# Second layer's modulation: all 48 rows on VectorE during the first feed-forward, instead of 16 on TensorE in the filter stage

## The chip, the cores and the metric

The kernel runs on one core of a Trainium2 chip. The metric is the device time of one execution in microseconds. The core has five engines that run their own instruction streams in order and meet at semaphores: PE (TensorE, matmuls), DVE (VectorE), ACT (ScalarE), POOL (GpSimd) and SP (SyncE, which here only issues transfers). Transfers are also issued by ACT and POOL.

## The reference, cut to what matters

Two layers over 512 latent and 256 context tokens of width 1024. Each layer takes six modulation vectors per stream from the conditioning vectors: one matrix-vector product per stream with a 1024 x 6144 matrix.

```python
sc = jax.nn.silu(c)
scc = jax.nn.silu(c_ctx)
for layer in range(DEPTH):
    mod_l = jnp.split((sc @ ada_w[layer] + ada_b[layer])[:, None, :], N_MOD, axis=-1)
    mod_c = jnp.split((scc @ ada_w[layer] + ada_b[layer])[None, None, :], N_MOD, axis=-1)
    h_l = rmsnorm(x, norm1_g[layer]) * (1.0 + mod_l[1]) + mod_l[0]
    h_c = rmsnorm(ctx, norm1_g[layer]) * (1.0 + mod_c[1]) + mod_c[0]
    # layer 0: SSD + Hyena mixer; layer 1: windowed attention
    x = x + mod_l[2] * o_l
    h_l = rmsnorm(x, norm2_g[layer]) * (1.0 + mod_l[4]) + mod_l[3]
    x = x + mod_l[5] * swiglu(h_l, ffn_w_in[layer], ffn_w_out[layer])
    # the same for ctx in layer 0
```

With features on partitions, the 6144 values of a layer are 48 columns of 128 ("rows" of the modulation in the kernel's words), each for two streams. Layer 0's Hyena mixer also needs a filter that depends on no activation (a small MLP, a window, a norm and a Fourier-like transform). The kernel makes it first; here this is called the filter stage.

## The kernel before, in words

Weights come as a list of jobs of 1 MB (two halves of 512 KB, in three slots of SBUF, job g in slot g mod 3). SP loads the halves in the order of the list, and each load waits until PE has finished the same half of the job three places earlier. The order of the list is written out by hand in `weight_jobs`.

The kernel multiplies in float32 by splitting each weight and each activation into a high and a low part. For each half of a job DVE casts the weights to the high part (`split_high`, line 1704, called from `next_high`), POOL subtracts to get the low part (`low`, line 2255), and PE does three products for each tile (lines 530, 531, 535). There is one buffer for the high parts of a job's two halves. So DVE may cast half 0 of the next job only when PE has finished half 0 of this one, and PE needs the cast and POOL's subtraction by the time it has finished half 1.

The modulation is made in two ways:

- As jobs called "ada". A pair of them (2 MB) gives four columns for both streams, by 8 skinny matmuls with a 32-column stationary operand (function `ada`, line 597). Layer 0's 12 pairs are made so, and also the first 16 columns of layer 1, in 4 pairs. Eight pairs are made one after another inside the filter stage, at calls of `fill()`: after each of the three MLP layers, after the sixth tile of the first half of the filter (`c` is 0 or 1 for the two halves of 512 columns), after the second and the sixth tile of the second half, and twice in the transform of the first half. The other 8 pairs lie between the "uv" jobs that follow.
- As rows on DVE. Columns 16 to 47 of layer 1 are dot products that DVE makes in the first feed-forward (`mod_rows`, line 2100): ACT loads two transposed rows (1 MB, 128 partitions x 2 x 1024) into the buffer `MW` (`rows`, line 1539), and DVE multiplies and sums them with the spread conditioning vectors, four instructions for two rows and two streams. There is one such buffer. ACT issues the next load only when DVE's count `mod_done` says that the previous pair of rows is finished, and DVE waits for the load on `mod_in`.

The feed-forward of layer 0 has two halves. Each half has 11 "up" jobs (two blocks of 8 tiles each) and then 8 "down" jobs (one block of 6 + 5 tiles). The program calls an up job with what the other engines do for it a turn; turns are counted 0 to 10. DVE's program in a turn of an up job is: cast half 0 and half 1 of the next job's weights (`next_high`), multiply the gate with the second block (line 2118), subtract to get the low part of the hidden tile (line 2120), and then `mod_rows`. ACT's is: issue the load of rows, SiLU of the first block (line 1546), copy of the hidden tile (line 1550). In the first half the turns 1 to 10 take the pairs 0 to 9, in the second half the turns 0 to 5 take the pairs 10 to 15. DVE's program for the down jobs begins with a memset (line 2037) in the second half and then the same casts.

In the filter stage the tile loop (lines 680, 1715, 1716) multiplies six tiles for each `c`, and the transform loop (line 717) follows with six steps. A step waits for DVE's result of two steps earlier (`kd_ev`), and the first two steps of the second tile loop wait for the last transform step of the first half.

## Time and profile before

| what | us |
|---|---|
| median of 3 runs | 2204.93 (2204.57 to 2212.95) |
| profiled execution, its own time | 2205.47 |
| its span | 2203.6 |
| PE busy | 2094.3 (95%) |
| DVE busy | 939.0 (43%) |
| POOL busy | 815.7 (37%) |
| ACT busy | 442.6 (20%) |

The span is the time from the first to the last instruction of the profiled execution; about 1.9 us of its own time lie outside. PE is the busy engine throughout, and the chain of waits that ended last lies 86% on PE. In the stretches where it lies elsewhere, an engine's share over the whole span says nothing; there the order of instructions and what each waits for have to be read.

### The profile page before, as it was taken

To read this page: it belongs to the slowest core of one execution; us is meant where nothing else is said; L and a number is where in the kernel's file an instruction comes from. 1 tells how busy PE (TensorE), PEld (TensorE's weight loads), DVE (VectorE), ACT (ScalarE), POOL (GpSimd) and SP (SyncE) were. 2 spreads that over 40 slices of the span, in tenths; PEclk is the share of its full clock that TensorE was granted. 3 is DMA by queue.
4 is the path that set the end of the run, shared out by engine and by line. 5 is a ranking of instruction groups with operands and counts; after the bars stand their busy time and mean duration, and the time that the engine had idled before them with its cause. 6 is when DMAs were issued, how large, how long until landed. Compare 5 with 4: busy or idle time off the path is not lost.

```text
span 2203.6 us, 29482 instructions
## 1 busy us (share of the span) xinstructions
PE 2094.3 (95%) x11738; PEld 1676.1 (76%) x11738; DVE 939.0 (43%) x1373; ACT 442.6 (20%) x831; POOL 815.7 (37%) x438
## 2 busy tenths in 40 slices
PE   7999999999988999999999999997989999999997
PEld 2477668888876778888888888886766677888886
DVE  4543545203347763335441353233446663322334
ACT  3331110012434550040100001103026602100110
POOL 1443646122247764242322323234210135444442
PEclk9999999999989999999999999999989999999999
DMA  9444321111110012123332232122200022223222
GB/s 391 160 148 149 117 94 48 39 58 48 39 37 2 1 60 87 58 67 115 139 105 70 96 115 83 46 72 78 67 29 1 1 76 82 85 86 110 95 76 77
DMA packets 50681, 182.31 MB, mean 83 GB/s; under 512 B 5329, under 2 KB 5841, under 8 KB 49425
## 3 DMA queue, kind: packets, MB, share of 16 engines
q1 hardware_dynamic: 45136, 156.32, 21.0%
q10 hardware_dynamic: 4928, 21.57, 2.6%
q0 software_dynamic: 512, 2.95, 0.4%
q8 instruction: 75, 1.23, 0.2%
q14 instruction: 30, 0.24, 0.0%
HBM read 178.72 MB, written 2.10 MB: 82 GB/s over the span
## 4 chain that ended last, share of the span: by engine, by line
PE 86%; DVE 5%; POOL 4%; DMA 2%; issue 2%; ACT 1%; SPq 0%; ACTq 0%; DVEq 0%; POOLq 0%
PE psum L530 21%; PE psum L535 21%; PE psum L531 21%; PE psum L1161 2%; PE psum L1149 2%; DMA weights<-in_wall 2%; PE psum L1178 2%; PE psum L717 1%; POOL weights_lo L2255 1%; PE psum L753 1%; PE psum L680 1%; PE psum L929 1%; PE psum L597 1%; PE psum L954 1%; DVE normed L1952 1%
## 5 line engine op out<-in xcount | busy, mean ns | idle before, releaser
L2255 POOL TENSOR_TENSOR weights_lo<-weights,weights_hi 128x1024 fp32r<-128x1024 f32 (+1 forms) x224 | 496.6, 2218 | 977.7 <-DVE weights_hi L1704 977.7
L535 PE MATMUL psum<-normed_lo,weights_hi 128*128 128x512 f32 x1760 | 505.5, 350 | 0.0
L1704 DVE CAST weights_hi<-weights 128x1024 fp32r<-128x1024 f32 (+1 forms) x228 | 162.5, 713 | 782.0 <-PE psum L535 707.3
L530 PE MATMUL psum<-normed_hi,weights_hi 128*128 128x512 f32 x1088 | 392.1, 360 | 7.4 <-DVE weights_lo L1800 4.6
L531 PE MATMUL psum<-normed_hi,weights_lo 128*128 128x512 f32 x1088 | 371.6, 356 | 0.0
L535 PEld LDWEIGHTS psum<-normed_lo,weights_hi 128*128 128x128 f32 x1760 | 282.3, 188 | 16.5
L530 PEld LDWEIGHTS psum<-normed_hi,weights_hi 128*128 128x128 f32 x1088 | 204.7, 188 | 57.9 <-DVE weights_lo L1800 4.3
L530 PE MATMUL psum<-normed_first_hi,weights_hi 128*128 128x512 f32 (+1 forms) x672 | 230.8, 343 | 4.9 <-DVE weights_lo L1800 2.6
L531 PEld LDWEIGHTS psum<-normed_hi,weights_lo 128*128 128x128 f32 x1088 | 205.1, 188 | 34.1 <-issue 1.0
L531 PE MATMUL psum<-normed_first_hi,weights_lo 128*128 128x512 f32 (+1 forms) x672 | 212.0, 337 | 0.0
L530 PE MATMUL psum<-hidden_hi,weights_hi 128*128 128x512 f32 (+1 forms) x528 | 189.0, 358 | 0.0
L531 PE MATMUL psum<-hidden_hi,weights_lo 128*128 128x512 f32 (+1 forms) x528 | 178.8, 354 | 0.0
L535 PE MATMUL psum<-hidden_lo,weights_hi 128*128 128x512 f32 (+1 forms) x528 | 160.3, 358 | 0.0
L530 PEld LDWEIGHTS psum<-normed_first_hi,weights_hi 128*128 128x128 f32 x672 | 126.7, 189 | 37.2 <-issue 5.7
L531 PEld LDWEIGHTS psum<-normed_first_hi,weights_lo 128*128 128x128 f32 x672 | 126.8, 189 | 16.0 <-issue 1.0
L530 PEld LDWEIGHTS psum<-hidden_hi,weights_hi 128*128 128x128 f32 x528 | 99.1, 188 | 23.5
L531 PEld LDWEIGHTS psum<-hidden_hi,weights_lo 128*128 128x128 f32 x528 | 99.3, 188 | 15.1
L1546 ACT ACTIVATE temps<-psum 128x768 f32<-128x768 f32 (+1 forms) x44 | 31.1, 707 | 375.5 <-PE psum L535 271.7
L1812 DVE SCALAR_TENSOR_TENSOR temps<-psum,vectors,temps 128x511 f32<-128x511 f32 x112 | 63.8, 612 | 94.5 <-ACT temps L1342 93.5
L1550 ACT ACTIVATE hidden_hi<-temps 128x768 fp32r<-128x768 f32 (+2 forms) x44 | 32.6, 740 | 313.5 <-DVE temps L2118 313.5
L535 PEld LDWEIGHTS psum<-hidden_lo,weights_hi 128*128 128x128 f32 x528 | 87.0, 188 | 8.9
L2120 DVE TENSOR_TENSOR hidden_lo<-temps,hidden_hi 128x768 fp32r<-128x768 f32 (+2 forms) x44 | 64.8, 1473 | 39.7 <-ACT hidden_hi L1550 39.7
(331 smaller groups left out, 3067.9 us busy)
## 6 DMA issues: line engine op xcount, KB each, us to landing
weights<-in_wall SPq DMA_DIRECT2D x232, 512.0 KB, 3.9
phase<-in_modw ACTq DMA_DIRECT2D x16, 1024.0 KB, 6.5
weights<-in_wall SPq DMA_DIRECT2D x32, 384.0 KB, 3.2
weights<-in_wall SPq DMA_DIRECT2D x32, 320.0 KB, 3.1
residual<-in_xT SPq DMA_DIRECT2D x1, 3072.0 KB, 16.4
phase<-in_tab ACTq DMA_DIRECT2D x2, 1280.0 KB, 5.5
residual<-in_xT ACTq DMA_DIRECT2D x1, 1920.0 KB, 7.2
normed<-in_window SPq DMA_DIRECT2D x1, 1536.0 KB, 13.5
```

What stands on the lines that cost most here:

```text
L530: mm(acc[:, lo:hi], WH[:, b, k, :], high[:, lo:hi], start=st, stop=False)
L531: mm(acc[:, lo:hi], WL[:, s, HALF * b + k, :], high[:, lo:hi], start=False, stop=False)
L535: ins = mm(acc[:, lo:hi], WH[:, b, k, :], low[:, lo:hi], start=False, stop=en)
L1149: ins = mm(PSF[:, 1024 * e + at0:1024 * e + at1], QT[rows, 2 * g + j, b * P:b * P + P], KD[rows, g, key:key + at1 - at0], start=c in (0, 2 ...
L1161: ins = pe.transpose(PSF[:, 2048 + t * P:2048 + t * P + P], EX[:, n % 4, 1 + t * P:1 + t * P + P], C[:, IDENT, :])
L1178: ins = mm(PS[64 * e:64 * e + 64, 6, 0:256].rearrange("p (j c) -> p j c", j=2), VT[:, kt, 64 * g:64 * g + 64], heads_e, start=t == 0, stop ...
L1546: run(T[:, 0, lo:hi], pair(0)[:, lo:hi], ACT.Silu).then_inc(pair_free[0], 1)
L1550: run(at_row(HIDH, r)[:, lo:hi], T[:, 1, lo:hi], ACT.Copy).then_inc(hid_hi, 1)
L1704: dve.tensor_copy(high_home(gs[0])[:, b, 0:n, :], W[:, s, HALF * b:HALF * b + n, :]).then_inc(w_hi, 1)
L1812: ins = STT(t[:, a:e], p[:, a + shift:e + shift], w, t[:, a:e], ALU.mult, ALU.add)
L2120: TT(at_row(HIDL, r)[:, lo:hi], T[:, 1, lo:hi], at_row(HIDH, r)[:, lo:hi].bitcast(f32), ALU.subtract).then_inc(hid_ready, 1)
L2255: TT(WL[:, s, at, :], W[:, s, at, :], high_home(gs[0])[:, b, 0:width(gs[0], b), :].bitcast(f32), ALU.subtract).then_inc(w_lo, 1)
```

## The change

The 8 ada jobs of layer 1 (four pairs, 8 MB of loads) leave the list of jobs. Of the eight `fill()` calls in the filter stage four remain: after the MLP's first two layers, after the sixth tile of the first half, and after the transform's step 3 of the first half. The group of psum rows that collects early pairs closes after four pairs (`LAST_AT`). The array of transposed rows in memory holds all 48 rows, 24 pairs, and `row_pairs` says which turn takes which: in the first half turns 1 to 10 take one pair each (0 to 9), in the second half turns 0 to 7 take one each (10 to 17), and turns 8, 9 and 10 take two each (18 to 23). The first pair's load of a turn is issued by ACT at the turn's start, as before; the second one's is issued by ACT after its copy of the hidden tile, again when DVE has finished the pair before. The gain of layer 1's first norm, made from those columns, moves behind the feed-forward.

```diff
-    ada1 = [("ada", 1, n) for n in range(24)]
-    stage("ada_a", ada0[:8] + ada1[:8])
+    stage("ada_a", ada0[:8])
...
+def row_pairs(half, r):
+    if half == 0:
+        return (r - 1,) if r else ()
+    return (10 + r,) if r < 8 else (2 * r + 2, 2 * r + 3)
...
                 ins.then_inc(mlp_mm, 1)
-                fill()
+                if layer < 2:
+                    fill()
...
-                    if t == 5 or c and t == 1:
+                    if t == 5 and c == 0:
                         fill()
...
-                    if n in (3, 5):
+                    if n == 3:
                         fill()
...
+                    def rows_in(pairs):
+                        for n in pairs:
+                            act.wait_ge(mod_done, n + 1)
+                            act.dma_start(MW, A["modw"][:, 2 * n:2 * n + 2, :]).then_inc(mod_in, 16)
...
-                        n = r - 1 + half * FH
-                        if n < 16:
-                            act.wait_ge(mod_done, n + 1)
-                            act.dma_start(MW, A["modw"][:, 2 * n:2 * n + 2, :]).then_inc(mod_in, 16)
+                        rows_in(row_pairs(half, r)[:1])
...
                         run(at_row(HIDH, r)[:, lo:hi], T[:, 1, lo:hi], ACT.Copy).then_inc(hid_hi, 1)
+                        if layer == 0:
+                            rows_in(row_pairs(half, r)[1:])
...
-                        mods(0, 0, 16)
-                        mods(1, 0, 16).then_inc(mods_a, 1)
+                        mods(0, 0, 16).then_inc(mods_a, 1)
...
             gains(1, 0, 4, "n2").then_inc(pair_free[2], 1)
-            gains(2, 1, 1, "n1")
...
-                n = r - 1 + half * FH
-                if n >= 16:
-                    return
-                dve.wait_ge(mod_in, 16 * (n + 1))
+                for n in row_pairs(half, r):
+                    dve.wait_ge(mod_in, 16 * (n + 1))
...
+                if half and r == FH - 1:
+                    dve.wait_ge(mod_done, 25)
...
             feed_forward(0, 1, SEGS)
-            dve.wait_ge(mod_done, 17)
+            dve.wait_ge(mod_done, 25)
+            gains(2, 1, 1, "n1")
             gains(3, 1, 4, "n2")
```

The first place is PE's order in the filter stage, from the transform's last two and a half steps of the first half to the transform's step 0 of the second half. In the kernel before (line 597 is an ada pair, 680 a tile's two matmuls, 717 the transform):

```order
L717 MATMUL psum<-phase 128x512 x6
L597 MATMUL psum<-weights,phase 32x512 x8
L680 MATMUL psum<-phase 128x512 x4
L597 MATMUL psum<-weights,phase 32x512 x8
L680 MATMUL psum<-phase 128x512 x8
L597 MATMUL psum<-weights,phase 32x512 x8
L717 MATMUL psum<-phase 128x512 x4
L608 MATMUL psum<-phase,normed 128x16 x4
```

In the changed kernel the same place (689 is the tile loop, 726 the transform):

```order
L726 MATMUL psum<-phase 128x512 x6
L689 MATMUL psum<-phase 128x512 x12
L726 MATMUL psum<-phase 128x512 x4
L616 MATMUL psum<-phase,normed 128x16 x4
L726 MATMUL psum<-phase 128x512 x4
```

Three ada pairs have left; the six tiles of the second half follow each other, and the transform follows them. The fourth pair that leaves stood between the MLP's third layer and the first tile.

The second place is DVE's order at the end of the up jobs of the second half. In the kernel before, from the second cast of turn 9 through turn 10 to the memset of the down jobs (a wait is on the semaphores in brackets):

```order
L1704 CAST weights_hi<-weights 128x1024 [waits w_loaded11,blocks_done]
L2118 TENSOR_TENSOR temps<-temps,psum 128x768 [waits pair_free0]
L2120 TENSOR_TENSOR hidden_lo<-temps,hidden_hi 128x768 [waits hid_hi]
L1704 CAST weights_hi<-weights 128x768 [waits w_loaded20,blocks_done,hid_ready]
L1704 CAST weights_hi<-weights 128x640 [waits w_loaded21,blocks_done]
L2118 TENSOR_TENSOR temps<-temps,psum 128x768 [waits pair_free0]
L2120 TENSOR_TENSOR hidden_lo<-temps,hidden_hi 128x768 [waits hid_hi]
L2037 MEMSET temps 128x768 [waits hid_ready]
```

In the changed kernel the end of turn 10 (line 2110 is `mod_rows`; each dot product is a pair of rows here):

```order
L2132 TENSOR_TENSOR hidden_lo<-temps,hidden_hi 128x768 [waits hid_hi]
L2110 ISA temps,mods<-phase,vectors 128x1024 [waits mod_rows_in,hid_ready]
L2110 ISA mods 128x1
L2110 ISA phase,mods<-phase,vectors 128x1024 [waits dve_order]
L2110 ISA mods 128x1
L2110 ISA temps,mods<-phase,vectors 128x1024
L2110 ISA mods 128x1
L2110 ISA phase,mods<-phase,vectors 128x1024
L2110 ISA mods 128x1
L2110 ISA temps,mods<-phase,vectors 128x1024 [waits mod_rows_in]
L2110 ISA mods 128x1
L2110 ISA phase,mods<-phase,vectors 128x1024 [waits dve_order]
```

Before, nothing stood between the subtraction of a turn and the casts of the next one in turns 6 to 10. Now turns 6 and 7 have four dot products there, and turns 8 to 10 have eight, with a second wait for `mod_rows_in` in their middle.

The third place is ACT's order at the same turns. In the kernel before, turns 8 to 10 hold only these:

```order
L1546 ACTIVATE temps<-psum 128x768 [waits pair_free1,blocks_done]
L1550 ACTIVATE hidden_hi<-temps 128x768 [waits v_in,pair_free1]
L1546 ACTIVATE temps<-psum 128x768 [waits pair_free1,blocks_done]
L1550 ACTIVATE hidden_hi<-temps 128x768 [waits v_in,pair_free1]
L1333 ACT_TABLE_LOAD
```

In the changed kernel:

```order
L1541 DMA phase<-in_modw 128x2x1024 [waits mod_rows_done]
L1558 ACTIVATE temps<-psum 128x768 [waits pair_free1,blocks_done]
L1562 ACTIVATE hidden_hi<-temps 128x768 [waits v_in,pair_free1]
L1541 DMA phase<-in_modw 128x2x1024 [waits mod_rows_done] x2
L1558 ACTIVATE temps<-psum 128x768 [waits pair_free1,blocks_done]
L1562 ACTIVATE hidden_hi<-temps 128x768 [waits v_in,pair_free1]
L1541 DMA phase<-in_modw 128x2x1024 [waits mod_rows_done] x2
L1558 ACTIVATE temps<-psum 128x768 [waits pair_free1,blocks_done]
L1562 ACTIVATE hidden_hi<-temps 128x768 [waits v_in,pair_free1]
L1541 DMA phase<-in_modw 128x2x1024 [waits mod_rows_done]
```

The "x2" is the second pair of one turn and the first pair of the next, each with its own wait for DVE, ahead of that next turn's SiLU.

## Rows read from the trace of the kernel before

**Rows 1.** Page: span, PE and DVE busy us, share.

```profile
span 2203.6 us, 29482 instructions
PE 2094.3 (95%) x11738; PEld 1676.1 (76%) x11738; DVE 939.0 (43%) x1373; ACT 442.6 (20%) x831; POOL 815.7 (37%) x438
```

**Rows 2.** Chain of waits, filter stage: start us, duration us, what.

```profile
26.26 4.05 PE psum L597 x12
...
66.58 1.57 ACT phase L1288 x2
...
73.77 2.35 PE psum L597 x16
...
83.19 1.85 PE psum L597 x16
```

**Rows 3.** Timeline, filter stage: start, duration, instruction, [idle before and its releaser].

```profile
29.04 0.06 DVE L1663 MEMSET phase<- 64x1 f32 x1
...
30.24 10.65 PE L680 MATMUL psum<-phase 128*128 128x512 f32 x24
```

**Rows 4.** Windows: us, busy by engine, PEclk, DMA share, GB/s.

```profile
28.00:30.00 2.00, 2.00 (x10) 0.19 (x4) 0.16 (x3) 0.84 (x1) 0.00 (x0) 0.56 0.99 417
...
948.00:950.00 2.00, 2.00 (x7) 1.62 (x7) 2.00 (x5) 1.97 (x4) 1.95 (x2) 0.50 0.00 0
950.00:952.00 2.00, 2.00 (x10) 1.78 (x8) 2.00 (x5) 1.97 (x5) 1.95 (x2) 0.66 0.00 0
```

**Rows 5.** Timeline of PE after a wait of 3.35 us.

```profile
947.82 0.65 PE L553 MATMUL psum<-normed_hi,weights_hi 128*128 128x512 f32 x1 [3.35 <-ACT normed_hi L1281]
```

**Rows 6.** Timeline of DVE, second half of the filter.

```profile
73.81 0.69 DVE L1715 TENSOR_TENSOR phase<-psum,normed 128x512 f32<-128x512 f32 x1 [0.33 <-PE psum L680]
...
78.07 0.69 DVE L1715 TENSOR_TENSOR phase<-psum,normed 128x512 f32<-128x512 f32 x1 [2.38 <-PE psum L680]
...
87.57 1.82 DVE L1704 CAST weights_hi<-weights 128x1024 fp32r<-128x1024 f32 x2
```

**Rows 7.** Timeline of DVE, up and down jobs of the first feed-forward.

```profile
1299.31 1.52 DVE L2120 TENSOR_TENSOR hidden_lo<-temps,hidden_hi 128x768 fp32r<-128x768 f32 x1 [0.91 <-ACT hidden_hi L1550]
1300.87 1.28 DVE L2100 CUSTOM_DVE_ANT_0 temps<-phase,vectors 128x1024 f32<-128x1024 f32 x1
...
1305.83 0.69 DVE L1704 CAST weights_hi<-weights 128x1024 fp32r<-128x1024 f32 x1
...
1372.26 0.70 DVE L1704 CAST weights_hi<-weights 128x1024 fp32r<-128x1024 f32 x1 [4.43 <-PE psum L535]
1380.58 0.69 DVE L1704 CAST weights_hi<-weights 128x1024 fp32r<-128x1024 f32 x1 [7.62 <-PE psum L535]
...
1389.01 0.70 DVE L1704 CAST weights_hi<-weights 128x1024 fp32r<-128x1024 f32 x1 [4.44 <-PE psum L535]
...
1417.53 0.70 DVE L2037 MEMSET temps<- 128x768 f32 x1 [0.23 <-DVE hidden_lo L2120]
1420.48 0.56 DVE L1704 CAST weights_hi<-weights 128x768 fp32r<-128x768 f32 x1 [2.25 <-PE psum L535]
1425.62 0.49 DVE L1704 CAST weights_hi<-weights 128x640 fp32r<-128x640 f32 x1 [4.58 <-PE psum L535]
```

**Rows 8.** Timeline of ACT's queue, an up job.

```profile
1305.94 0.37 ACTq L1539 DMA_DIRECT2D phase<-in_modw  x1
```

**Rows 9.** Timeline of POOL, an up job and the first down job's weights.

```profile
1306.60 2.42 POOL L2255 TENSOR_TENSOR weights_lo<-weights,weights_hi 128x1024 fp32r<-128x1024 f32 x1 [6.57 <-DVE weights_hi L1704]
...
1406.39 1.85 POOL L2255 TENSOR_TENSOR weights_lo<-weights,weights_hi 128x768 fp32r<-128x768 f32 x1 [5.89 <-DVE weights_hi L1704]
```

**Rows 10.** Line 1539: its 16 loads of rows, issue to landing.

```profile
DMA to landing us min/median/max: 4.9/6.5/7.2
```

**Rows 11.** Timeline of DVE, end of the first feed-forward.

```profile
1508.15 1.48 DVE L1676 SCALAR_TENSOR_TENSOR gains<-mods,vectors 128x16 f32<-128x16 f32 x1
...
1511.06 0.23 DVE L1776 RECIPROCAL temps<-temps 128x12 f32<-128x12 f32 x1 [1.43 <-ACT temps L1267]
```

More of the change, by code:

```diff
@@ L106 @@
 PLAN = plan()
-PAIR = {g: n for n, g in enumerate([g for g, job in enumerate(JOBS) if job[0] == "ada"][::2])}
+PAIR = {g: n if n < 4 else n + 4
+        for n, g in enumerate([g for g, job in enumerate(JOBS) if job[0] == "ada"][::2])}
+LAST_AT = (3, 7)
+def row_pairs(half, r):
+    if half == 0:
+        return (r - 1,) if r else ()
+    return (10 + r,) if r < 8 else (2 * r + 2, 2 * r + 3)
 G0 = AT["out0"]
@@ L598, in ada @@
                                      W[:, s, 8 * b + 4 * k:8 * b + 4 * k + 4, :].rearrange("p a c -> p (a c)"),
-                                     start=part == 0 and at == 0, stop=part == 1 and at == 7)
+                                     start=part == 0 and at == 0, stop=part == 1 and at == LAST_AT[group])
                         ins.then_inc(blocks_done, 1)
@@ L1310, in _ @@
                 if c:
-                    copy_row(0, AT["ada_a"] + 14)
+                    copy_row(0, AT["ada_a"] + 6)
                 for m in range(6):
@@ L1550, in up @@
                         run(at_row(HIDH, r)[:, lo:hi], T[:, 1, lo:hi], ACT.Copy).then_inc(hid_hi, 1)
-                        if layer == 0 and half == 0 and isinstance(r, int) and r == 0:
+                        if layer == 0:
+                            rows_in(row_pairs(half, r)[1:])
+                        if layer == 0 and half == 0 and r == 0:
                             act.wait_ge(flipped, 3)
@@ L2092, in mod_rows @@
                     return
-                n = r - 1 + half * FH
-                if n >= 16:
-                    return
-                dve.wait_ge(mod_in, 16 * (n + 1))
-                for q in range(2):
-                    m = 16 + 2 * n + q
-                    for j in range(2):
-                        ins = dve.tensor_tensor_reduce(MW[:, q, :] if j else WASTE, MW[:, q, :], SPREAD[:, j, :], 1.0, vec("ada_b", 48 + m),
-                                                       ALU.mult, ALU.add, MOD[:, 1, m, j:j + 1])
-                        if q == j == 0:
-                            ch.link(ins)
-                ins.then_inc(mod_done, 1)
+                for n in row_pairs(half, r):
+                    dve.wait_ge(mod_in, 16 * (n + 1))
+                    for q in range(2):
+                        m = 2 * n + q
+                        for j in range(2):
+                            ins = dve.tensor_tensor_reduce(MW[:, q, :] if j else WASTE, MW[:, q, :], SPREAD[:, j, :], 1.0,
+                                                           vec("ada_b", 48 + m), ALU.mult, ALU.add, MOD[:, 1, m, j:j + 1])
+                            if q == j == 0:
+                                ch.link(ins)
+                    ins.then_inc(mod_done, 1)
+                if half and r == FH - 1:
+                    dve.wait_ge(mod_done, 25)
             def feed_forward(layer, n, segs):
@@ L2596, in _layout @@
         "wall": wall.reshape(len(JOBS), P, JT * P), "vec": vec,
-        "modw": a["ada_w"][1][:, 16 * P:].T.reshape(32, P, D).transpose(1, 0, 2),
+        "modw": a["ada_w"][1].T.reshape(48, P, D).transpose(1, 0, 2),
         "xT": xt.reshape(KT, P, TOK).transpose(1, 0, 2), "w_dt": wdt.reshape(KT, P, 32).transpose(1, 0, 2),
```

## The prediction, made before the changed kernel ran

> **What bounds the kernel now.** I read the page first: PE is busy 95% of the span, DVE 43% [rows 1]. A share over the whole span prices nothing here, because the change takes work from one short stage and puts work into another. So I read the chain of waits in the filter stage, to see which of the ada pairs that leave are on it. The reader is to see that the pairs at 73.77 and 83.19 us are (2.35 and 1.85 us), that the one at 26.26 us is part of the chain's start, and that at 66.58 us the chain runs through ACT's squares while a pair is done beside it [rows 2]. Then I read one up job of the first feed-forward on DVE, ACT and POOL, engine by engine. There PE waits for nobody, and the question is how much time lies between DVE's last instruction of a turn and the moment PE needs the weights that DVE casts next.
>
> **Filter stage, what leaves.** Four ada pairs.
>
> The pair at 73.77 us. Before it, tile 1 of the second half reached DVE at 73.81; tile 2 reached it at 78.07 [rows 6]. The four matmuls of a tile take PE 10.65 / 6 = 1.78 us [rows 3], so without the pair tile 2 arrives 78.07 - 2.35 or so: gain 2.35 us.
>
> The pair at 83.19 us. Behind it PE goes on with the transform's step 0, whose inputs DVE has ready. DVE's casts of the first uv job (87.57, 1.82 us long) [rows 6] come 2.35 us earlier too and end before the result of step 1 reaches DVE, so they cover nothing. Gain 1.85 us.
>
> The second pair in the transform of the first half. The chain passes it on ACT (squares at 66.58) [rows 2]; PE did the pair while it would have waited. Gain 0. I know no way in which its absence hurts.
>
> The pair at 26.26 us. The first tile needs DVE's memset, 29.04 + 0.06, and started at 30.24 because of the pair [rows 3]. So it could start 1.0 us earlier. But the granted clock was 0.56 between 28 and 30 us [rows 4], and the pair's matmuls were what kept PE busy. Without them PE is idle for some 6 us before the first tile. After an idle stretch of 3.35 us [rows 5] the clock was 0.50 for 2 us and 0.66 in the next 2 [rows 4]: half rate (1.2 instead of 2.4 GHz) for about 2 + 2 x 0.68 = 3.4 us, which costs PE half of it, 1.7 us. So this pair is worth between +1.0 (no effect of the clock) and -1.0 us (a little longer at half rate). I take a loss of 0.5, nearer to the row.
>
> Sum of the filter stage: 2.35 + 1.85 - 0.5 = 3.7 us gained, bounds 2.3 and 5.2. The upper one is 2.35 + 1.85 + 1.0; the lower takes the loss of 1.0 and 0.9 more for the load of x, which is now issued behind job 7 and so behind the pair at the end of the first six tiles (about 41 us), not at 28.6. ACT squares it from about 56 us.
>
> The Trainium skill ("TensorE: Matmul & The Clock Gate", section "HAM oscillation — how this bites in real kernels") says that a wait on a transfer throttles the array again and that the work behind it starts cold. The rows above agree, with 0.50 granted after 3.35 us of idle. Without this effect the sum would be 5.2; it is in my term, from rows.
>
> **Filter stage, what goes with it.** `mods(1, 0, 16)` is one small DVE instruction beside PE's work: 0. The loads that go (8 MB): the jobs up to the first tile are loaded as before, later ones aren't waited for before either: 0.
>
> **Second layer's gain, moved.** It now stands at the end of the first feed-forward, beside one of the same shape that takes 1.48 us there at 1508.15. DVE is then idle for 1.43 us before 1511.06 [rows 11]. The new one fits in the gap: 0; if it took the full 1.48 again, 0.05.
>
> **First feed-forward, turns 6 and 7 of the second half.** They get one pair of rows each, as the turns 1 to 10 of the first half had. Four dot products take from 1300.87 to 1305.83, that is 4.96 us [rows 7]. A turn is 1389.01 - 1372.26 = 16.75 us. PE finishes half 0 in phase with the cast at 1372.26, half 1 with that at 1380.58, 8.32 us later [rows 7]. With a pair in each turn the cast starts at 1305.83, and 1372.26 - 4 x 16.75 = 1305.26 is when it could have: 0.57 late. POOL's part follows at 1306.60 and ends at 1309.02 [rows 9], while PE needs it at 1305.26 + 8.32 = 1313.58. The slack is 4.5 us. So these two turns cost 0.
>
> **Turns 8 to 10, two pairs each.** The second pair is loaded into the same buffer, so ACT may issue it only when the first is finished, and DVE stands at `mod_in` until it has landed. Behind DVE's wait are the casts for the next job; POOL and PE wait for those. A load takes 4.9 to 7.2 us, median 6.5 [rows 10]. ACT issues it 0.11 us after DVE's last dot product (1305.94 against 1305.83) [rows 7, 8]. I lay it out in the old time scale; L is a load.
>
> Turn 8. DVE ends its first pair at 1305.83 + 5 x 16.75 = 1389.58, 0.57 after PE's half 0 at 1389.01. Load issued 1389.7, L = 6.5 as in the same phase before, landed 1396.2, second pair until 1401.2. Cast, and POOL 0.77 after the cast's start (1306.60 - 1305.83) for 2.42: 1404.4. PE needed it at 1389.01 + 8.32 = 1397.3. PE stands 7.1 us.
>
> Turn 9. ACT issues the next load (pair 20) at 1401.3, L = 4.9, since no weights are being loaded; it lands at 1406.2, which is when DVE has done two casts, the product and the subtraction (about 4.8 us with ACT's SiLU and copy between). Pair until 1411.2; second load, L = 5.7 (between), landed 1417.0; pair until 1422.0. The next weights are the first down job's, 768 wide: POOL starts 0.63 behind the cast and takes 1.85 [rows 9], so 1424.5. PE did its job in 16.75 us from 1404.4, plus 1.7 for a clock at half rate after 7.1 us of idle: 1422.9. PE stands 1.6 us.
>
> Turn 10. Load issued 1422.1, L = 6.5, landed 1428.6; pair until 1433.6; second load, L = 5.7, landed 1439.4; pair until 1444.4; memset 0.70 [rows 7]; cast and POOL 0.63 + 1.85: 1447.6. PE's down job is short, from half 0 at 1414.03 to 1420.48 and 1425.62 in the old scale [rows 7], where 1414.03 is 1389.01 + 16.75 + 8.32 less 0.05. So it runs from 1424.5 to 1436.0, and PE stands 11.6 us.
>
> The second down job started at 1425.6 and now starts at 1447.6: 22.0 us late (7.1 + 1.7 + 1.6 + 11.6). After 11.6 us idle the clock comes back at half rate, 1.7 to 3 us; I take 1.8. DVE has no rows left and catches up within one job. Sum 23.8 us lost.
>
> With every L at 4.9 the five loads are shorter by 1.6, 0, 0.8, 1.6 and 0.8, so the delay is 17.2 us, and 19.0 with the clock. With every L at 7.2 they are longer by 0.7, 2.3, 1.5, 0.7 and 1.5, and the delay is 28.7, or 31.7 with 3 us for the clock.
>
> **Sum.** Profiled execution 2205.47 - 3.7 + 23.8 = 2225.6. The median of the runs lies 0.54 below the profiled execution, so 2225 us. The cheap ends: 2204.93 - 5.2 + 19.0 = 2218.7. The dear ends: 2204.93 - 2.3 + 31.7 = 2234.3; five loads at the longest of sixteen are unlikely together.
>
> **Rivals.**
>
> A. Not slower: the double turns are hidden. For it: DVE stands idle 4.43 to 7.62 us before each cast in turns without rows [rows 7], in all about 12 us a turn, and two pairs take 9.9. Against it: this idle lies ahead of casts that wait for PE, not behind, and the load in the middle isn't work that can overlap. It decides from the point where 4.96 + L fits into the slack of 4.5 us, which no L does. Then 2204.93 - 3.7 = 2201 us, inside 0.5%. Chance 0.05.
>
> B. Only DVE's own time counts, since the loads are on the way while DVE still works (the order would have to let ACT pass DVE's count). Each double turn then ends 0.57 + 4.96 = 5.5 us late, 0.4 us more than 0.57 + 4.5 allow; behind turn 10 the down job gives only 11.5 us, and DVE and POOL need from half 1 on 4.0 + 9.9 + 0.7 + 2.5 = 17.1, 5.6 too many. So 2204.93 - 3.7 + 6 = 2207 us. For it: nothing in ACT's order. Against: each of the two loads waits for DVE's count. Chance 0.03.
>
> C. Each stall costs its own cold start on top. By my layout the half rate after the first stall is swallowed by the second, since DVE and the loads, not PE, set when the next weights are there. If instead the loads are fast and PE sets it, the first and second stall cost 1.7 each on the end: 2225 + 1.7 + 1.7 = 2228 us. The Trainium skill's section named above speaks for it (every tile behind a wait starts cold); the rows fix only the size of one start. Chance 0.1, still slower.
>
> D. The filter stage loses too: x lands late, and squares, POOL's sums and the transform wait. Job 7, x and the second window are 5.5 MB; at 417 GB/s [rows 4] they take 13 us from 41 us on and land about 54 to 56, when x is needed. 3 us more at worst: 2204.93 + 3 + 23.8 = 2232 us. Chance 0.04.
>
> The forecast itself has the rest, 0.78. About 0.5% (11 us) is what a measurement of this kernel can tell from no change. Slower by more than that (above 2216): forecast, C and D, 0.92, less a little for luck with L: 0.91. Within 0.5%: A and B, 0.08. Faster by more: 0.01. Range 2217 to 2232: it leaves out A and B and the farthest dear end.
>
> **What would show it.** In the profile after: PE idle before a down job's first product of about 11 us, released by POOL's weights_lo, and 7 us before the last up job; idle of DVE before the dot products, released by the load of rows, in turns 8 to 10, of 5 to 7 us for each second pair; 24 loads of rows, 8 more. Granted clock 0.5 after the two long stalls. In the filter stage the first tile starts near 29.2 at a granted clock of 0.5, and PE's first uv product near 108.5 instead of 112.19. I am wrong if PE shows no wait above 2 us in the second half's up jobs, or if the filter stage isn't 2 to 5 us shorter.

## The result, and the profile after

The changed kernel takes 2229.2 us (median of 4 runs, 2228.09 to 2232.97); the kernel before, run on the same chip, takes 2206.06 us. The ratio is 1.0097, with a 95% interval of 1.0082 to 1.0113: slower by 1%, or 21.4 us (0.0097 x 2206.06). The forecast was 2225 us in a range of 2217 to 2232.

The page of the changed kernel, span and busy times. They answer to [rows 1].

```profile
span 2226.2 us, 29374 instructions
PE 2091.8 (94%) x11674; PEld 1679.7 (75%) x11674; DVE 983.4 (44%) x1436; ACT 442.7 (20%) x831; POOL 817.4 (37%) x438
```

PE has 64 matmuls and 2.5 us less to do, and the span is 22.6 us longer: the time is in waits. DVE gains 44.4 us of work (eight more pairs of rows), which by itself says little: five of the eight pairs cost almost nothing, as the first experiment shows.

PE's waits after: engine and line, what it waited for, us in total, times, longest.

```profile
PE psum L538 <- POOL weights_lo L2268: 21.9, 5, 11.9
PE psum L689 <- DVE phase L1677: 5.9, 1, 5.9
```

Two of the five waits behind the first line lie at the end of the first feed-forward's up jobs: 7.23 and 11.87 us. The other three come to 2.8 us, as much as the kernel before has on the same tile. Between the two long ones lies a third, of 1.34 us, that the view files under "issue"; POOL's subtraction of 1.82 us that started at 1422.09 ended 0.10 us before this product, so the same chain set it. The timeline of PE there: start, duration, instruction, [idle before and its releaser].

```profile
1403.67 0.80 PE L538 MATMUL psum<-normed_hi,weights_hi 128*128 128x512 f32 x1 [7.23 <-POOL weights_lo L2268]
1424.01 0.47 PE L538 MATMUL psum<-hidden_hi,weights_hi 128*128 128x512 f32 x1 [1.34 <-issue]
1447.67 0.77 PE L538 MATMUL psum<-hidden_hi,weights_hi 128*128 128x512 f32 x1 [11.87 <-POOL weights_lo L2268]
```

The same three matmuls in the kernel before, where nothing waits:

```profile
1397.12 0.40 PE L530 MATMUL psum<-normed_hi,weights_hi 128*128 128x512 f32 x1
1413.87 0.40 PE L530 MATMUL psum<-hidden_hi,weights_hi 128*128 128x512 f32 x1
1425.42 0.40 PE L530 MATMUL psum<-hidden_hi,weights_hi 128*128 128x512 f32 x1
```

They are 6.55, 10.14 and 22.25 us late.

POOL is only the last link. Its own wait in the same turns is for DVE's cast, and DVE's waits are for the rows. The timelines of DVE, ACT's queue and POOL, turns 8 to 10, some instructions of each; they answer to [rows 7 to 9].

```profile
1395.17 1.28 DVE L2110 CUSTOM_DVE_ANT_0 temps<-phase,vectors 128x1024 f32<-128x1024 f32 x1 [6.38 <-DMA phase<-in_modw]
1400.12 1.29 DVE L1718 CAST weights_hi<-weights 128x1024 fp32r<-128x1024 f32 x2
1405.28 2.46 DVE L2110 CUSTOM_DVE_ANT_0 temps<-phase,vectors 128x1024 f32<-128x1024 f32 x1 [0.85 <-DMA phase<-in_modw]
1416.51 1.28 DVE L2110 CUSTOM_DVE_ANT_0 temps<-phase,vectors 128x1024 f32<-128x1024 f32 x1 [5.01 <-DMA phase<-in_modw]
1422.71 1.55 DVE L1718 CAST weights_hi<-weights 128x640 fp32r<-128x640 f32 x1 [0.70 <-PE psum L543]
1427.03 1.28 DVE L2110 CUSTOM_DVE_ANT_0 temps<-phase,vectors 128x1024 f32<-128x1024 f32 x1
1438.63 1.28 DVE L2110 CUSTOM_DVE_ANT_0 temps<-phase,vectors 128x1024 f32<-128x1024 f32 x1 [6.57 <-DMA phase<-in_modw]
...
1444.91 0.96 DVE L1718 CAST weights_hi<-weights 128x768 fp32r<-128x768 f32 x2 [0.32 <-DVE temps L2049]
```

```profile
1388.83 11.78 ACTq L1541 DMA_DIRECT2D phase<-in_modw  x2
1411.52 10.42 ACTq L1541 DMA_DIRECT2D phase<-in_modw  x2
1432.10 0.37 ACTq L1541 DMA_DIRECT2D phase<-in_modw  x1
```

```profile
1400.89 5.76 POOL L2268 TENSOR_TENSOR weights_lo<-weights,weights_hi 128x1024 fp32r<-128x1024 f32 x2 [17.98 <-DVE weights_hi L1718]
...
1445.55 4.21 POOL L2268 TENSOR_TENSOR weights_lo<-weights,weights_hi 128x768 fp32r<-128x768 f32 x2 [19.62 <-DVE weights_hi L1718]
```

What they show is a closed loop: DVE's last dot product frees the single buffer (1388.71 + 0.09), ACT issues the next load 0.03 us later (1388.83), the rows land after 6.3 us, and only then does DVE go on to the second pair and to the casts queued behind it. Every second pair waits 5.0 to 6.6 us for its load.

The windows around the two long waits: us, busy by engine, PEclk, DMA share, GB/s.

```profile
1406.00:1408.00 2.00, 2.00 (x7) 1.71 (x7) 1.97 (x3) 0.00 (x0) 0.66 (x1) 0.50 0.02 4
1408.00:1410.00 2.00, 2.00 (x13) 1.72 (x13) 2.00 (x3) 0.00 (x0) 0.00 (x0) 1.00 0.00 0
...
1452.00:1454.00 2.00, 2.00 (x12) 1.70 (x11) 0.00 (x0) 0.00 (x0) 0.00 (x0) 0.91 0.00 0
```

PE came back at 1.2 GHz (0.50) and stayed there for 4.3 us after the first wait (1403.67 to 1408) and for about 4.7 us after the last (1447.67 to 1452.4, from the 0.91 of the last window).

Four landmarks give the account between the two profiles (after minus before): PE's first uv product -2.82 us; DVE's cast for half 1 of turn 8 -0.85 (1379.73 against 1380.58 [rows 7]); the last cast of the feed-forward +24.46 (1530.94 against 1506.48); the end +22.6. So turns 8 to 10 cost 25.3 us, the filter stage gave 2.8, and some 2 us of that gain went and came back at waits that both kernels have (last section).

The filter stage, by the chain of waits: start, duration, what. It answers to [rows 2, 3].

```profile
28.81 12.44 PE psum L689 x24
41.24 1.86 PE psum L605 x16
...
52.44 3.17 PE psum L706 x16
...
58.47 3.70 PE psum L726 x8
...
71.70 10.62 PE psum L689 x24
82.32 3.53 PE psum L726 x8
```

And the same steps in the chain of the kernel before, so far as they don't stand in [rows 2].

```profile
30.31 10.58 PE psum L680 x24
40.89 1.85 PE psum L597 x16
...
52.09 1.92 PE psum L697 x16
...
56.86 3.70 PE psum L717 x8
...
70.10 3.67 PE psum L680 x8
...
85.04 3.63 PE psum L717 x8
```

From the second half's first tile to the transform behind the tiles, before takes 85.04 - 70.10 = 14.94 us and after 82.32 - 71.70 = 10.62: the two pairs were worth 4.32. But that first tile starts 1.60 late (71.70 against 70.10), and this is already there at 58.47 against 56.86. It is made of 0.35 in the first tiles (41.24 against 40.89: 1.50 earlier, 1.86 longer) and 1.25 in L706, the norms' products, which take 3.17 instead of 1.92. There PE's clock is down, as the windows of after show:

```profile
52.00:54.00 2.00, 1.56 (x10) 1.03 (x11) 0.56 (x4) 0.37 (x2) 0.00 (x0) 0.73 1.16 498
54.00:56.00 2.00, 2.00 (x9) 1.14 (x8) 0.30 (x1) 0.00 (x0) 0.00 (x0) 0.50 0.87 375
```

### The profile page after: what moved, and what is told of

It is laid out like the page before. It is cut to its first block, busy times and chain, and to the rows that moved or that the text cites. A ratio compares the mean times of both kernels' runs of the same rounds, so it can differ in the third digit from the quotient of the medians.

```text
span 2226.2 us, 29374 instructions
## 1 busy us (share of the span) xinstructions
PE 2091.8 (94%) x11674; PEld 1679.7 (75%) x11674; DVE 983.4 (44%) x1436; ACT 442.7 (20%) x831; POOL 817.4 (37%) x438
## 4 chain that ended last, share of the span: by engine, by line
PE 83%; DVE 6%; POOL 4%; issue 3%; DMA 2%; ACT 2%; DVEq 0%; ACTq 0%; SPq 0%; POOLq 0%
PE psum L538 20%; PE psum L543 20%; PE psum L539 20%; PE psum L1170 2%; PE psum L1158 2%; PE psum L1187 2%; PE psum L726 1%; PE psum L762 1%; DMA weights<-in_wall 1%; POOL weights_lo L2268 1%; PE psum L689 1%; PE psum L938 1%; PE psum L963 1%; DVE normed L1964 1%; PE psum L815 1%
## 5 line engine op out<-in xcount | busy, mean ns | idle before, releaser
L538 PE MATMUL psum<-normed_hi,weights_hi 128*128 128x512 f32 x1088 | 392.9, 361 | 13.8 <-POOL weights_lo L2268 10.0
L538 PEld LDWEIGHTS psum<-normed_hi,weights_hi 128*128 128x128 f32 x1088 | 205.4, 189 | 65.2 <-POOL weights_lo L2268 11.8
L538 PE MATMUL psum<-normed_first_hi,weights_hi 128*128 128x512 f32 (+1 forms) x672 | 231.8, 345 | 4.4 <-ACT phase L1407 2.4
L538 PE MATMUL psum<-hidden_hi,weights_hi 128*128 128x512 f32 (+1 forms) x528 | 190.2, 360 | 13.2 <-POOL weights_lo L2268 11.9
L538 PEld LDWEIGHTS psum<-normed_first_hi,weights_hi 128*128 128x128 f32 x672 | 127.2, 189 | 37.2 <-issue 6.3
L538 PEld LDWEIGHTS psum<-hidden_hi,weights_hi 128*128 128x128 f32 x528 | 99.9, 189 | 37.4 <-issue 13.8
```

The source lines that it names most:

```text
L538: mm(acc[:, lo:hi], WH[:, b, k, :], high[:, lo:hi], start=st, stop=False)
```

## The experiments

All ratios are to the kernel before on the same chip, with their 95% interval. The first four take the double turns apart.

**e1_one_pair.** One pair in each turn of the second half, so that no turn is double; the last three pairs (rows 42 to 47 of the modulation) are left out and set to zero.

```
-    return (10 + r,) if r < 8 else (2 * r + 2, 2 * r + 3)
+    return (10 + r,)
```

> The changed kernel with one pair of rows in each of the turns 8 to 10 of the second half instead of two; rows 42 to 47 of the second layer's modulation are left out (set to zero). Theory W (the second load and its products behind one another in a turn, ahead of the next casts, stop PE): all of the loss goes and only the filter stage's gain is left: 2203 us, 2200 to 2206, no PE wait on weights_lo above 1 us in up or down jobs. Rival E (the loss comes from the change elsewhere: slots, the moved gain, other loads): stays within 5 us of 2229.

Measured 2206.55 us (10 runs), 0.9985 (0.9975 to 0.9995). That is 0.55 us above the expected range; the kernel before took 2209.67 us beside it, 3.6 more than beside the changed kernel, so that the ratio is the better measure. In the first feed-forward no wait of PE for POOL's weights reaches 1 us. So the slowdown belongs to the three second pairs: by ratios 1.0097 - 0.9985 = 0.0112, or 24.7 us. What is left is a gain of 0.15%.

**e2_no_second_load.** Double turns keep both pairs' products, but the second pair works on the data that the first had (rows 38, 39, 42, 43, 46 and 47 are computed from wrong data); no load stands between them.

```
-                        if layer == 0:
-                            rows_in(row_pairs(half, r)[1:])
...
+                        if n % 2:
+                            dve.wait_ge(mod_done, n + 1)
```

> The changed kernel without the three second loads: the second pair's products are made on the data of the first, right behind it (rows 38, 39, 42, 43, 46, 47 are made from the wrong data). Theory W says that each double turn is then 0.57 + 4.96 us late against 5.1 us that the up jobs forgive, and 5.4 us too late only for the second down job: 0.5 + 0 + 5.4 us of PE waits, about 1.7 for the clock, 2211 us (2208 to 2214). Rival D (DVE's own time is what costs): within 4 us of 2229.

Measured 2213.89 us (10 runs), 1.0018 (1.0006 to 1.0029). PE's timeline at the two places where it waits:

```profile
1400.47 0.51 PE L538 MATMUL psum<-normed_hi,weights_hi 128*128 128x512 f32 x1 [0.55 <-POOL weights_lo L2272]
...
1434.91 0.77 PE L538 MATMUL psum<-hidden_hi,weights_hi 128*128 128x512 f32 x1 [5.87 <-POOL weights_lo L2272]
```

These are rival B's waits, 0.4 and 5.6 by its working. The time is at the upper end of the expected range. B is thus right about DVE's time and wrong about the kernel: with the loads in the loop the waits are 7.23, 1.34 and 11.87.

**e3_load_only.** The other half: the second load is there, but its products are left out (DVE waits for it and counts on; the same rows are zero).

```
+                    if half and r >= 8 and n % 2:
+                        dve.memset(MARK[:, 0:1], 0.0).then_inc(mod_done, 1)
+                        continue
```

> The changed kernel with the three second loads but without the products on them (rows 38, 39, 42, 43, 46, 47 are set to zero); DVE waits for each load as before. Theory W: PE waits of about 2 us before the last up job, 0 before the first down job, 6 before the second, with 1.7 for the clock: 2213 us (2209 to 2217). Rival D: no loss beyond the filter gain, 2203 us. Rival L (the load's round trip is nearly all of the cost): above 2220 us.

Measured 2218.54 us (6 runs), 1.0043 (1.0028 to 1.0057).

```profile
1397.27 0.50 PE L538 MATMUL psum<-normed_hi,weights_hi 128*128 128x512 f32 x1 [2.21 <-POOL weights_lo L2273]
1415.61 0.47 PE L538 MATMUL psum<-hidden_hi,weights_hi 128*128 128x512 f32 x1 [1.32 <-issue]
...
1434.35 0.77 PE L538 MATMUL psum<-hidden_hi,weights_hi 128*128 128x512 f32 x1 [6.92 <-POOL weights_lo L2273]
```

Against e1, the products alone cost 0.33% (7.3 us), the loads alone 0.58% (12.8 us), both together 1.12% (24.7 us). They don't add up because each alone first uses the same slack. Turn 8 shows it: 0.55 us of PE's wait with the products alone, 2.21 with the load alone, and 0.55 + 2.21 + 4.5 of slack is 7.26, where both together give 7.23. The time was 5.5 us above the 2213 expected, and 1.5 above the range. Of the 5.5, 3.6 are the base (e1 took 2206.55 beside it, not 2203); the rest is in the waits, 10.5 us in all where 8 were expected, 1.3 of it in a second wait expected at 0. The clock had its 1.7 in the expectation; it was at 0.50 from 1432 to 1436 and 0.56 to 1438.

**e4_before_double.** The kernel before with its filter stage untouched, and in it the double turns alone (16 rows are made a second time with the same values).

```
+    return (10 + r,) if r < 8 else (2 * r + 2, 2 * r + 3)
...
+                            at = 2 * (n % 16)
+                            act.dma_start(MW, A["modw"][:, at:at + 2, :]).then_inc(mod_in, 16)
```

> The kernel before with its filter stage and all its jobs untouched, and in the second half of the first feed-forward eight more pairs as in the changed kernel (turns 6 and 7 one, 8 to 10 two), which make sixteen rows a second time with the same result. Theory W: the first feed-forward alone costs 24 to 27 us, so 2206 + 25 = 2231 us (2228 to 2234), above the changed kernel by the filter stage's 1 to 4 us. Rival E: 2206 us.

Measured 2235.06 us (4 runs), 1.0118 (1.0092 to 1.0144): +26 us, as expected by the ratio, while the time is 1 us above the range with its base of 2206. PE's last wait is 12.65 us.

```profile
1406.98 0.79 PE L537 MATMUL psum<-normed_hi,weights_hi 128*128 128x512 f32 x1 [6.94 <-POOL weights_lo L2268]
...
1451.68 0.76 PE L537 MATMUL psum<-hidden_hi,weights_hi 128*128 128x512 f32 x1 [12.65 <-POOL weights_lo L2268]
```

The double turns need nothing of the rest of the change to do their harm: by the ratios they cost 26 us here and 24.7 against e1, and the rest gives back 0.15% (e1) to 0.21% (this run against the changed kernel), 3 to 5 us. The second of these differences is not clear of zero: both intervals together allow some 0.3% either way. Within the intervals the two halves of the change add up.

The cost can also be read inside each profile, without the filter stage, from DVE's cast for half 1 of turn 8 to its last cast of the feed-forward. In the kernel before these are 1380.58 and 1506.48:

| profile | from | to | us | against before |
|---|---|---|---|---|
| before | 1380.58 | 1506.48 | 125.90 | |
| e1, one pair a turn | 1381.03 | 1508.09 | 127.06 | 1.2 |
| e2, products alone | 1383.21 | 1517.81 | 134.60 | 8.7 |
| e3, loads alone | 1378.35 | 1517.79 | 139.44 | 13.5 |
| changed kernel | 1379.73 | 1530.94 | 151.21 | 25.3 |
| e4 | 1383.33 | 1535.41 | 152.08 | 26.2 |

Against e1 the products alone cost 7.5, the loads alone 12.4, both 24.1 us, close to the 7.3, 12.8 and 24.7 of the ratios. The 1.2 us of e1 belong to its pair in turn 10, ahead of the short down job: PE waits 0.68 us there, at 1426.71, for POOL's weights. So the up turns take one pair each for nothing, and the last of them not quite.

e4 has the filter stage of before, and so shows what varies in it from one profile to the next. Its chain has, at the norms' products,

```profile
52.17 2.93 PE psum L704 x16
```

where before has 1.92, and its first uv product stands at 112.94, not 112.19.

**v1_rows_in_down.** All 24 pairs again and no turn double: four of them go behind the down jobs 1, 3, 5 and 7 of the first half, the up turns 0 to 9 of the second half take one each. From here on every kernel computes everything.

```
-    return (10 + r,) if r < 8 else (2 * r + 2, 2 * r + 3)
+    return (14 + r,) if r < 10 else ()
...
+                        if name == "down00" and r % 2:
+                            row_products((10 + r // 2,))
```

> The changed kernel with all 24 pairs, none doubled: four of them (10 to 13) behind the down jobs 1, 3, 5 and 7 of the first half, the others one in each up turn (second half: turns 0 to 9). Theory W: no PE wait on weights_lo above 0.5 us in the first feed-forward; all of the loss goes and the filter stage's gain stays, 0.998 to 0.9995 of the kernel before, like the run with one pair in each turn. Rival S (a pair in a down job is too long for it, since the job is only 11.5 us): PE waits of 1 us or more in each of the four down jobs and no gain.

Measured 2204.63 us (11 runs), 0.9981 (0.9969 to 0.9993). PE's waits for POOL's weights at L538 are three of 2.8 us in all, the longest 0.9, as in the kernel before, and none of them lies in the first feed-forward. The stretch of the table takes 125.90 us (1381.11 to 1507.01), as before; rival S is out. The 48 rows are free if they are spread: the loss was the placing, three turns that had to take six pairs, and not the amount of work on DVE. It gains as much as e1 does without its last three pairs.

The other three look for the filter stage's missing gain. **v2_fill_layer2** is v1 with the pair from behind the sixth tile put back behind the filter MLP's last layer, where the kernel before had it (the load of x with it).

```
-                if layer < 2:
-                    fill()
+                fill()
...
-                    if t == 5 and c == 0:
-                        fill()
```

> As the kernel with rows in the down jobs, and the early ada pair behind the sixth tile of the first half moved back to behind the MLP's third layer, where the kernel before has one. Theory C: PE works at 25 to 30 us, the first tiles run at the full clock more of the time, 1.85 us leave the path behind the sixth tile, and the first tile starts 1.4 us later. First uv product at 107 to 109 us. Rival: the clock has no part in it, so the sum is -1.85 + 1.4 = -0.45 us against the changed kernel's 109.4 to 110.8: 109 to 110.4.

Measured 2201.92 us (11 runs), 0.9971 (0.9959 to 0.9983); first uv product 109.45. That is outside the 107 to 109 of theory C and inside the 109 to 110.4 of its rival. But the clock did have a part, against both: the norms' products (L703) took 3.57 us where before has 1.92, and the second half's tiles started at half rate,

```profile
70.08 12.32 PE L688 MATMUL psum<-phase 128*128 128x512 f32 x24 [2.33 <-DVE phase L1766]
```

where the changed kernel has 10.62 behind the same wait of 2.33 us. Without these two, 1.65 and 1.70 us, the product would stand at 106.1 by my estimate. The interval of the ratio overlaps v1's.

**v4_fill_n5** is v1 with the pair at the transform's step 3 moved to step 5.

```
-                    if n == 3:
+                    if n == 5:
```

> As the kernel with rows in the down jobs, and the last early ada pair moved from the transform's step 3 of the first half to its step 5, where PE waits for ACT's squares anyway. Theory C (with no pair there PE stands open for 2.3 us, and its clock sometimes falls there): the pair costs nothing in its new place, 1.85 us less on the path, and the clock never falls between 70 and 84 us. The first uv product at 107.5 to 109 us. Rival: it is worth 1.85 us only because of its place and the clock falls as before; first uv product between 107.5 and 113.

Measured 2204.9 us (12 runs), 0.9983 (0.997 to 0.9996), the same as v1; first uv product 110.91, a miss for theory C and inside its rival's 107.5 to 113. The timeline shows why: ACT waits for x, which SP issued at 45.67.

```profile
62.94 0.84 ACT L1297 ACTIVATE temps<-residual 128x768 f32<-128x768 f32 x1 [2.88 <-DMA residual<-in_xT]
...
73.24 3.24 PE L689 MATMUL psum<-phase 128*128 128x512 f32 x7 [2.82 <-DVE phase L1769]
```

With the pair gone from PE's chain, ACT's squares of x are next. x lands at 62.9, the squares and POOL's sums between them take until PE's tile at 73.24, and the 1.85 us gained on PE are spent waiting. Behind this wait of 2.82 us the clock held, 1.00 from 70 to 84 us, so that this half of theory C stands in this profile.

**v3_fill_layer2_n5** makes both moves.

> Both moves together: the four early ada pairs stand behind the MLP's three layers and at the transform's step 5 of the first half. Theory C: first uv product at 112.2 - 2.35 - 3 x 1.85 = 104.3 us (104 to 106), no fall of the clock between 36 and 84 us beyond what the kernel before shows, and a time of 0.995 to 0.998 of the kernel before, the fastest of all. Rival: what is gained in the filter stage is lost again before the first feed-forward, since waits of 3 to 4 us there meet the clock in another phase; then 0.998 to 1.0.

Measured 2199.91 us (9 runs, 2193.6 to 2203.84), 0.9958 (0.9943 to 0.9973): 0.4% under the kernel before and the lowest median of all. Its interval overlaps v2's for the most part and v1's a little, so that which of the two moves made the gain over v1 isn't settled. The chain of waits in its filter stage:

```profile
30.73 10.58 PE psum L688 x24
...
50.59 1.92 PE psum L703 x16
...
67.17 4.13 PE psum L688 x9
```

Neither loss of the changed kernel is left in this profile: the first tiles take 10.58 and the norms' products 1.92, both at full clock. x is issued at 29.45 and squared at 54.94 without a wait, so that the second half's tiles start at 67.17 (2.93 before those of the kernel before), and the first uv product stands at 104.84, 7.35 earlier than 112.19.

## Why the prediction was right, by its steps

The sign and the mechanism are as forecast, and the sizes are near. By profiles the forecast was 20.1 us more and 22.6 came: 1.5 more in turns 8 to 10 (25.3 against 23.8) and 0.9 less gained in the filter stage (2.8 against 3.7). The other 1.6 us between 2225 and 2229.2 are the median's place beside the profiled execution, taken as 0.5 below it and measured 1.1 above.

**The loop of one buffer** (the step that made the sign). Right in place and in size: PE's waits were laid out as 7.1, 1.6 and 11.6 us and are 7.23, 1.34 and 11.87. e2 and e3 show that it takes both halves of the loop, and e1 that nothing else of the change slows the kernel by more than its interval. The agreement to a few tenths is in part luck, since the single pieces differ and cancel: from issue to DVE's next product the loads took 6.3, 5.0, 5.0 and 6.5 us where I had 6.5, 4.9, 5.7 and 5.7, and the first pair of turn 10 started at 1427.03 without a wait, since its load came in under DVE's work. Against the shorter loads stand a dot product of 2.46 us in turn 9 and the cast at 1422.71, which took 1.55 us where before has 0.49 for the same cast (1414.07), both beside POOL's subtractions (last section).

**The clock after the waits.** Sizes too small: 1.7 and 1.8 us. PE's matmuls after against before tell it. The one ahead of the first wait stands 0.85 us early; 1403.67 is 6.55 late, the end of that job 8.64, the job behind the second wait 10.14 to 10.21, 1447.67 is 22.25 late and the feed-forward's last cast 24.46. So the waits cost 7.4, 1.6 and 12.0 us from start to start (each 0.2 more than the idle that the view gives), and the half rate 2.1 and 2.2, about half of its 4.3 and 4.7 us. Sum 25.3 instead of 23.8, of which 0.8 is the clock and 0.7 the waits. The row I took it from [rows 4] had 3.4 us at half rate. Most of the first 2.1 is swallowed by the second wait, as the prediction said. A little of it may reach the end: DVE's cast at 1422.71 waited 0.70 us for PE, and the rows behind it could have started 0.5 us earlier, when their load had landed (4.9 us after its issue at 1421.57).

**Turns 6 and 7, moved gain: 0.** Right. PE has no wait there, and in the feed-forward's end both gains together take 1.57 us (1532.61), 0.09 more than the one did [rows 11].

**Pairs at 73.77 and 83.19 us: 2.35 + 1.85.** Right: 4.32 together, read off the two chains.

**Pair at 26.26 us: -0.5.** Right for the first tiles (-0.35). But that the first tile could start 1.0 earlier held in this profile (1.50), not in others. That tile now hangs on the filter MLP, and through it on the weights of the pair behind the MLP's second layer. It starts at 28.81, 29.83, 30.05, 30.10, 30.22 and 30.74 in the six profiles without the pair, and at 30.31, 30.39, 30.55 and 30.73 in the four with it. PE stood idle for 5.9 us ahead of it in all six, and its 24 matmuls took 12.44 to 13.21 us instead of 10.58. So the first tiles end at 41.24 in the changed kernel's profile and at 42.30 to 43.95 in the other five, against 40.89 to 41.31 in the four with the pair: the loss is 0.35 us in this profile and 1.4 to 3.1 in the others, outside the bound of 1.0. That the term came out near in the profile of the result was luck. This scatter makes most of the difference between the changed kernel's first uv product (109.37) and those of v1, e1 and e3 (110.39 to 110.79).

**Sum of the filter stage: 3.7.** The profile has 2.82. The term is mis-sized by the 1.25 us at L706, but the change is hardly to blame: e4 has the same slow products in the old filter stage, and of the ten profiles only that of before and that of v3 have 1.92. The profile of before that I worked from was a good one. Against e4's 112.94, the changed kernel gains 3.6, and v1, e1 and e3 2.2 to 2.6. But e2, which has the same filter stage, has its first uv product at 114.98 and loses 2.0 (next paragraphs). The times say 0.15% for e1 (3.3 us, interval 1.1 to 5.5, and 1.2 more if the cost of its turn 10 is added back) and 0.19% for v1 (4.2 us, 1.5 to 6.8). So a gain is shown, and 3.7 lies in the middle of what the times allow; single profiles scatter by more than the term.

**"I know no way in which its absence hurts"** (the second pair in the transform). Too strong as a sentence: e2 shows a possible one, in one execution. PE waits 3.04 us before the tiles, and starts them at half rate (0.50 granted from 74 to 78 us): 13.56 us for the 24 matmuls instead of 10.62.

```profile
46.93 17.13 DMA residual<-in_xT
...
74.37 13.56 PE L689 MATMUL psum<-phase 128*128 128x512 f32 x24 [3.04 <-DVE phase L1765]
```

In the changed kernel the same wait is 2.33 us and the clock holds; in v2 it is 2.33 us too and the clock falls. Before, PE does a pair of 1.85 us there. That the missing pair is the cause isn't shown by a run of its own: v4 has a pair there again, PE still waits 2.82 us behind it, and the clock holds.

**Rival D, x late.** Half of it came: x was issued at 44.08, not at about 41, and ACT waited 2.65 us for it, to 61.17, where the prediction had it land at 54 to 56. But it cost nothing in this profile. In the chain ACT was 1.60 late at 67.69 against 66.09, before it came to the squares, and 1.60 late behind them. In e2, with the same filter stage, it did come: the first line above is the load of x, issued at 46.93 and landed at 64.06, and it stands in the chain of waits. That is one of the five profiles of this filter stage. It cost 0.7 us there (PE's wait of 3.04 against 2.33) and perhaps the half rate behind it; the load was late because the pair ahead of it was, since the first tiles ended at 43.95 against 41.24. It bites too when PE's chain gets shorter, which is v4.

**Rival C** (its own cold start for each stall): no. PE's second wait is set by DVE and POOL; without the first cold start it would be about 2 us longer, and the second wait of 1.34 us brought no cold start of its own (0.47 us for the first product, 1.00 granted from 1422 to 1428).

What stays open: when the clock falls at 50 to 56 us and when it doesn't, and when it falls at the second half's tiles (e2 and v2 of ten). At 50 to 56 us it fell in eight profiles of ten, among them e4, whose pairs there stand as in the kernel before, and v2, whose pairs up to that point stand as in v3, where it held. How much of v3's 7.35 us in the filter stage is this luck (1.25 us at most are at L706) isn't settled by one profile; the ratio of 0.9958 over nine runs doesn't rest on it.

## What to carry to other kernels

Before putting more work into a turn that "has room", write down the loop that the work closes: who frees its buffer, who issues the load and what stands behind the wait in the same engine's order. A turn with 12 us of idle DVE could not take a second pair of 5 us, since its load started only when the first pair was done and the casts stood behind both; the same work spread so that no turn takes two (v1) cost nothing.

When work leaves a stage, ask of each piece what it covered: a late load, or a hole in PE's activity. Here the load of x stood behind one of the pairs, and moving that pair and another back to places that the kernel before had used gave the version with the lowest median.

## What the runs showed of the hardware

**The same wait is not the same clock.** PE waits 3.54 us for DVE in both kernels at 272 to 274 us, with the work shifted by 1.8 us. The timelines and a window each, of before and then of after:

```profile
273.84 1.55 PE L753 MATMUL psum<-phase 128*128 128x512 f32 x3 [3.54 <-DVE phase L1822]
...
274.00:276.00 2.00, 2.00 (x6) 1.00 (x7) 0.00 (x0) 0.14 (x1) 1.02 (x1) 1.00 0.95 291
```

```profile
272.07 3.78 PE L762 MATMUL psum<-phase 128*128 128x512 f32 x4 [3.54 <-DVE phase L1835]
...
274.00:276.00 2.00, 2.00 (x4) 0.95 (x3) 0.00 (x0) 0.11 (x1) 0.00 (x0) 0.50 0.70 285
```

Before, PE goes on at full rate, after, at half, until about 278 us. The wait of 2.33 us ahead of the second half's tiles has both outcomes as well (the changed kernel 10.62 us for the 24 matmuls, v2 12.32). The wait of 3.35 us at the start of the next stage (1517.62 before, 1542.78 after) doesn't: there the first product after it took 0.47 us before and 0.77 after, but before, the clock fell 0.4 us later and the third product took 0.63 (0.50 granted from 1518 to 1520).

In the ten profiles PE's waits of 5.8 to 12.7 us in the stages read here were followed by half rate each time; after 2.3 to 3.5 us the clock held in some and fell in others. That is how 2 us of the filter stage's gain were lost by turn 8, the stretch around 272 us above all. The 1.9 us came back behind the feed-forward in the same way: the work that before does at 0.50 from 1640 to 1644 us is done at 1.00 after, 24 us later (1664 to 1668). A gain of 2 to 3 us in an early stage can't be read off the end of one profile.

The Trainium skill ("TensorE: Matmul & The Clock Gate", section "HAM oscillation — how this bites in real kernels") says that work behind a long wait on a transfer starts cold each time. The long waits above agree (7.23 and 11.87 us, 0.50 granted behind both), though PE waited for POOL there, and the transfer lies further back in the chain; with the short ones the same wait of 3.54 us has both outcomes.

**DVE beside POOL.** The dot product at 1405.28 took 2.46 us, while POOL's subtractions ran from 1400.89 to 1406.65; the next one, at 1407.79 with POOL idle, took 1.28. POOL's two took 2.73 and 3.08, where the one in [rows 9] took 2.42. It lies inside the loop, ahead of turn 9's second load, so that up to 1.2 us of PE's wait of 1.34 in that turn may be its doing; no run takes it away alone. The cast at 1422.71 is a second case: 1.55 us beside POOL's subtraction of 1422.09 to 1423.91, 0.49 for the same cast before, with POOL idle.

The Trainium skill ("SBUF — State Buffer", section "Who interferes with whom") says that the two engines share a port pair under an exclusive lock, and that a DVE instruction with two inputs in SBUF contends for it with a GpSimd instruction that reads SBUF. If the second to start is blocked until the first has ended, the product would take 1406.65 - 1405.28 + 1.28 = 2.65 us, an estimate by that page's rule; the trace has 2.46, where POOL's ends are rough.
